# Latent heads scored by pairs with a 32-row rotary product, and banded-layer masks moved to the front of their turn

## The reference

```python
cq, ckv, kr = jnp.split(h @ w_a, [MLA_Q_LORA, MLA_Q_LORA + MLA_KV_LORA], axis=-1)   # 384, 256, 32
cq = rms_norm(cq, g_q); ckv = rms_norm(ckv, g_kv)
q = (cq @ w_uq).reshape(B, L, 16, 64 + 32); q_nope, q_rope = jnp.split(q, [64], axis=-1)
q_rope = apply_rope(q_rope, cos, sin); k_rope = apply_rope(kr[:, :, None, :], cos, sin)
kv = (ckv @ w_ukv).reshape(B, L, 16, 64 + 64); k_nope, v = jnp.split(kv, [64], axis=-1)
qf = concat([q_nope, q_rope]); kf = concat([k_nope, broadcast(k_rope, 16 heads)])
o = dense_causal_attention(qf, kf, v)          # logits over 96 rows, softmax, times v
return o.reshape(B, L, 1024) @ w_o
```

## Time and profile before

| what | value |
|---|---|
| median of 3 runs (lowest to highest) | 1332.93 us (1330.98 to 1333.79) |
| profiled execution: its time, its span | 1333.88 us, 1332.1 us |
| TensorE busy | 1296.4 us, 97% |
| VectorE, ScalarE, GpSimd busy | 938.3, 793.8, 225.8 us |
| TensorE granted clock, mean | 0.995 of full speed |

### The profile page before, as it was taken

The page is one execution under the profiler, slowest core; times in us unless marked ns, Lnnn a source line. Parts: engine busy times, 40 slices in busy tenths (PEclk is TensorE's granted clock), DMA queues, the critical chain, the costliest instruction groups (busy, mean ns, idle before and its releaser), DMA issues.

```text
span 1332.1 us, 29945 instructions
## 1 busy us (share of the span) xinstructions
PE 1296.4 (97%) x10381; PEld 1252.5 (94%) x10381; DVE 938.3 (70%) x1877; ACT 793.8 (60%) x1625; POOL 225.8 (17%) x208
## 2 busy tenths in 40 slices
PE   7999999999998999999998999999999999999997
PEld 7999999999887999999987899999999899999997
DVE  4765877765787877765678687776567667777665
ACT  4565666654565676664476667666446565766643
POOL 1000044420000034330001003433000000244300
PEclk9999999999999999999998999999999999999999
DMA  7432465556421455556442045555645334465562
GB/s 267 140 110 80 143 189 185 178 180 198 133 91 49 130 185 184 180 155 213 155 127 80 33 143 187 187 172 165 208 139 158 111 112 127 144 187 189 174 218 83
DMA packets 56723, 202.80 MB, mean 152 GB/s; under 512 B 6208, under 2 KB 8256, under 8 KB 56512
## 3 DMA queue, kind: packets, MB, share of 16 engines
q1 hardware_dynamic: 56640, 201.68, 47.4%
HBM read 200.61 MB, written 1.05 MB: 151 GB/s over the span
## 4 chain that ended last, share of the span: by engine, by line
PE 82%; DVE 7%; ACT 5%; issue 3%; DMA 1%; POOL 1%; ACTq 0%; DVEq 0%; POOLq 0%; SPq 0%
PE ps L385 23%; PE ps L389 22%; PE ps L388 22%; PE ps L535 2%; PE ps L553 2%; ACT probs L889 2%; DVE w_lo L1260 1%; PE ps L424 1%; PE ps L518 1%; PE ps L430 1%; PE ps L427 1%; ACT w_hi L839 1%; DMA raw<-in_weights 1%; POOL gated L1234 1%; DVE scores L1320 1%
## 5 line engine op out<-in xcount | busy, mean ns | idle before, releaser
L1260 DVE TENSOR_TENSOR w_lo<-raw,w_hi 128x1024 fp32r<-128x1024 f32 x377 | 461.1, 1225 | 230.3 <-ACT w_hi L839 228.9
L385 PE MATMUL ps<-h_hi,w_hi 128*128 128x272 f32 (+1 forms) x1752 | 508.6, 290 | 1.8 <-DVE q_rope L1526 1.0
L389 PE MATMUL ps<-h_hi,w_lo 128*128 128x272 f32 (+1 forms) x1752 | 505.8, 289 | 0.0
L388 PE MATMUL ps<-h_lo,w_hi 128*128 128x272 f32 (+1 forms) x1752 | 499.6, 285 | 0.0
L839 ACT ACTIVATE w_hi<-raw 128x1024 fp32r<-128x1024 f32 x377 | 395.0, 1050 | 147.7 <-PE ps L385 136.9
L385 PEld LDWEIGHTS ps<-h_hi,w_hi 128*128 128x128 f32 x1752 | 329.1, 188 | 8.4 <-issue 5.4
L388 PEld LDWEIGHTS ps<-h_lo,w_hi 128*128 128x128 f32 x1752 | 330.0, 188 | 0.3
L389 PEld LDWEIGHTS ps<-h_hi,w_lo 128*128 128x128 f32 x1752 | 328.9, 188 | 0.0
L385 PE MATMUL ps<-hid_hi,w_hi 128*128 128x272 f32 (+2 forms) x636 | 185.4, 292 | 2.2 <-DVE w_lo L1260 1.9
L388 PE MATMUL ps<-hid_lo,w_hi 128*128 128x272 f32 (+2 forms) x636 | 183.1, 288 | 0.0
L389 PE MATMUL ps<-hid_hi,w_lo 128*128 128x272 f32 (+2 forms) x636 | 183.0, 288 | 0.0
(11 more groups left out here) (184 smaller groups left out, 1727.3 us busy)
## 6 DMA issues: line engine op xcount, KB each, us to landing
raw<-in_weights SPq DMA_DIRECT2D x377, 512.0 KB, 3.7
cst<-in_consts SPq DMA_DIRECT2D x1, 1795.5 KB, 12.1
h<-in_x SPq DMA_DIRECT2D x2, 544.0 KB, 5.8
out<-h SPq DMA_DIRECT2D x8, 128.0 KB, 1.7
```

What stands on the lines that cost most here:

```text
L385: m = pe.matmul(b, whi, xhi, start=n == 0, stop=False)
L388: pe.matmul(b, whi, xlo, start=False, stop=False)
L389: m = pe.matmul(b, wlo, xhi, start=False, stop=n == len(tiles) - 1)
L1260: return dve.tensor_tensor(out_, a_, b_, op)
```

## The change

Latent layer: the nope rows of two heads lie on the two halves of the partitions, as in the other layers; the rotary rows of four heads share one tile, and the rotary key, whose 32 weight columns are laid out four times, lies on all four quarters. A pair's scores are six products of 64 rows and then six of 32 rows added to them. The copies under the heads go away (GpSimd has no part any more), copies by halves become whole ones, the key scale is spread from the per-token column by three small products in place of the ones-product, and the order of the first panels becomes rope, query, key, rope. Fox: `take_k` before the second split of its turn. Swa: masks first, split before `normalise`. Table load: from before the first splits of `down` to after those of its second panel.

```diff
-            def score(a, kind, hn):
-                q, key = queries[0:K_ROWS[kind], hn], keys[0:K_ROWS[kind], hn]
-                if hn >= 2:
-                    pe.wait_ge(masked, h0 + hn - 1)
...
+            def score_latent(a, m):
+                if m:
+                    pe.wait_ge(masked, HEADS * a + 2 * m)
                 for ch, (lo, hi) in enumerate(CHUNKS):
+                    hi_q = max(hi, P)
+                    for s in range(2):
+                        r = slice(HD * s, HD * s + HD)
+                        pe.matmul(ps[0:hi_q - lo, 2 + s, SCOL[ch]:SCOL[ch + 1]], queries[r, m, lo:hi_q],
+                                  keys[r, m, 0:hi], start=ch == 0, stop=False)
+                for ch, (lo, hi) in enumerate(CHUNKS):
+                    hi_q = max(hi, P)
+                    for s in range(2):
+                        t = MLA_ROPE * ((2 * m + s) % 4)
+                        r = slice(t, t + MLA_ROPE)
+                        ins = pe.matmul(ps[0:hi_q - lo, 2 + s, SCOL[ch]:SCOL[ch + 1]],
+                                        queries[r, PAIRS + m // 2, lo:hi_q], keys[r, PAIRS, 0:hi],
+                                        start=False, stop=ch == 2)
+                ins.then_inc(scored, 2)
@@ sum_squares, and after the swap of the rotary key
-                            if not is_q:
-                                pe.matmul(ps[:, 6, 0:T], ones, y[:, k % 4, :], start=k == ks[0], stop=k == ks[-1])
+                    pe.wait_ge(lat_scale, 1)
+                    for n, (lo, hi) in enumerate(((0, P), (P, 2 * P), (2 * P, T))):
+                        ins = pe.matmul(ps[:, 6, lo:hi], lat_col[0:hi - lo, 1, n:n + 1].broadcast_to([hi - lo, P]),
+                                        ident[0:hi - lo, 0:hi - lo], start=True, stop=True)
@@ ScalarE, latent
-                        for s in range(2):
-                            ins = act.activation(queries[0:HD, 2 * m + s, :], bank(p, 2)[HD * s:HD * s + HD], ACT.Copy)
-                        ins.then_inc(q_taken, 1)
+                        act.activation(queries[:, m, :], bank(p, 2), ACT.Copy).then_inc(q_taken, 1)
@@ ScalarE, output
-                if n % 2:
-                    act.preload_act_table_set(TABLES)
...
+                    if k == 1 and n % 2:
+                        act.preload_act_table_set(TABLES)
                     if k:
                         square(n, k - 1)
@@ GpSimd: the four copies of the rotary key are gone
@@ VectorE, fox
                             split_units(a, "qk", 0, 2 * m)
-                            if m == 0:
-                                take_k(m)
+                            take_k(m)
                             split_units(a, "qk", 0, 2 * m + 1)
-                            if m:
-                                take_k(m)
@@ VectorE, swa
-                    split_units(a, "vk", 0, 0)
                     for j in range(2):
                         dve.wait_ge(panel_done, pv + j + 1)
                         vk_evac(0, j, bank(pv + j), pv + j)
+                    split_units(a, "vk", 0, 0)
...
-                        if m >= 4:
-                            out_lo(a, m - 4)
                         if m >= 2:
                             mask_scores(a, kind, 2 * m - 4)
                             mask_scores(a, kind, 2 * m - 3)
                         if 1 <= m <= PAIRS:
                             rope_q(m - 1)
+                        if m >= 4:
+                            out_lo(a, m - 4)
+                        if m < PAIRS:
+                            split_units(a, "q", 0, m)
                         if m >= 2:
                             normalise(a, kind, 2 * m - 4)
                             normalise(a, kind, 2 * m - 3)
                         if m < PAIRS:
-                            split_units(a, "q", 0, m)
                             dve.wait_ge(panel_done, pq + m + 1)
@@ VectorE, mla
-                        for t in range(4):
-                            r = slice(32 * t, 32 * t + 32)
-                            ins = tt(queries[64:96, 4 * m + t, :], y[r, 0, :], y[r, 1, :], ALU.add)
-                        ins.then_inc(roped, 1)
+                        tt(queries[:, PAIRS + m, :], y[:, 0, :], y[:, 1, :], ALU.add).then_inc(roped, 1)
...
-                        tt(keys[0:64, 2 * m, :], b[0:64], kv_rstd[0:64], ALU.mult)
-                        tt(keys[0:64, 2 * m + 1, :], b[64:128], kv_rstd[64:128], ALU.mult).then_inc(bank_free, 2)
+                        tt(keys[:, m, :], bank(p, 2), kv_rstd, ALU.mult).then_inc(bank_free, 2)
...
-                    own.link(dve.reciprocal(kv_rstd, kv_rstd))
...
-                        if m:
-                            normalise(a, kind, 2 * m - 2)
                         if m < PAIRS:
                             take_k(m)
+                        normalise(a, kind, 2 * m - 2)
```

More of the change, by code:

```diff
@@ L266, in build_program @@
             sem(n) for n in ("lat_sq", "lat_sum", "lat_std", "lat_hi", "lat_scale"))
[L267 removed]
+        vt_done, vt_copied, q_taken, lat_spread = (
+            sem(n) for n in ("vt_done", "vt_copied", "q_taken", "lat_spread"))
         conv_begun, silu_done, gate_mul, hid_hi_done, hid_ready = (
@@ L787, in _ @@
                             swap_rope(n // 4)
-                    for r in range(2):
-                        panel(sq, uq, pq, 0, r, from_latent(0), None, 0)
-                    for m in range(PAIRS + 1):
+                    for j, first in ((0, 0), (1, 0), (2, QT)):
+                        panel(sq, uq, pq, 0, j, from_latent(first), None, 0)
+                    pe.wait_ge(q_taken, 1)
+                    panel(sq, uq, pq, 0, 3, from_latent(0), None, 0, pq + 1)
+                    for m in range(1, PAIRS + 1):
                         p = pq + 2 + 2 * m
@@ L1120, in _ @@
                     split_unit(uv + 1 + AHEAD)
[L1121 to L1124, removed]
+                    take_r(2)
+                    split_panel(a, "qk", 0)
+                    take_q(0)
+                    split_panel(a, "qk", 1)
+                    split_panel(a, "qk", 2)
+                    take_r(3)
+                    split_panel(a, "qk", 3)
+                    for m in range(1, PAIRS + 1):
                         if m >= 4:
                             out_hi(a, m - 4)
-                        if m:
-                            exps(a, kind, 2 * m - 2)
+                        exps(a, kind, 2 * m - 2)
                         if m < PAIRS:
                             take_q(m)
-                        if m:
-                            exps(a, kind, 2 * m - 1)
+                        exps(a, kind, 2 * m - 1)
                         if m < PAIRS:
@@ L1212, in _ @@
             for a, kind in enumerate(KINDS):
[L1213 to L1224, removed]
                 norm(2 * a, "o")
@@ L1602, in rope_key_rows @@
                         dve.wait_ge(bank_free, LAYERS[a]["a"][2] + 6)
-                        own.link(tt(scores[0:32, 0, 0:T], gated[0:32, :], cos[0:32], ALU.mult))
+                        one, two = scores[:, 0, 0:T], scores[:, 1, 0:T]
+                        own.link(tt(one, gated[:], cos, ALU.mult))
                         dve.wait_ge(swapped, base)
-                        tt(scores[0:32, 1, 0:T], ps[0:32, 7, 0:T], sin[0:32], ALU.mult).then_inc(roped, 1)
+                        tt(two, ps[:, 7, 0:T], sin, ALU.mult).then_inc(roped, 1)
                         dve.wait_ge(roped, base)
-                        tt(scores[0:32, 0, 0:T], scores[0:32, 0, 0:T], scores[0:32, 1, 0:T],
-                           ALU.add).then_inc(key_roped, 1)
+                        tt(keys[:, PAIRS, :], one, two, ALU.add).then_inc(key_roped, 1)
                     def rope_r(m):
-                        dve.wait_ge(bank_free, pr + m + 1)
+                        dve.wait_ge(bank_free, (pr, pr + 1, pq, pq + 3)[m] + 1)
                         dve.wait_ge(lat_sum, QT + KT)
@@ L1638, in _ @@
                     split_unit(uv + AHEAD)
[L1639 to L1640 removed]
                     rope_r(1)
                     split_unit(uv + 1 + AHEAD)
[L1643 to L1645 removed]
+                    dve.wait_ge(lat_std, 2)
+                    split_units(a, "qk", 0, 0)
+                    take_k(0)
+                    for j in (1, 2, 3):
+                        split_units(a, "qk", 0, j)
+                    for m in range(1, PAIRS + 1):
                         if m == PAIRS:
                             out_lo(a, m - 4)
[L1648 to L1650 removed]
+                        mask_scores(a, kind, 2 * m - 2)
+                        mask_scores(a, kind, 2 * m - 1)
                         if 4 <= m < PAIRS:
                             out_lo(a, m - 4)
[L1653 to L1654 removed]
                         if m < PAIRS:
                             take_k(m)
[L1657 to L1658 removed]
+                        normalise(a, kind, 2 * m - 2)
+                        normalise(a, kind, 2 * m - 1)
                         if m < PAIRS:
```

(6 more changed lines are left out.)

45 lines of the change are left out of this document (15 added, 30 removed).

## The result

| | before | after |
|---|---|---|
| median, us (13 runs each) | 1332.94 (1330.98 to 1335.41) | 1335.36 (1334.52 to 1338.27) |
| profiled execution: time, span | 1333.88, 1332.1 | 1334.52, 1332.3 |
| TensorE, VectorE, ScalarE, GpSimd busy | 1296.4, 938.3, 793.8, 225.8 | 1298.4, 923.9, 790.2, 221.3 |

The ratio is 1.0022, interval 1.0014 to 1.0029: 2.4 us slower against a forecast of 1.8 slower (1334.7). As I wrote, two halves nearly cancel; the stretches between the first matmuls of the four up projections separate them (each holds the MLP of one layer and the mixer of the next, which is named).

What follows compares the result with a forecast made beforehand. TensorE, 82% of the chain, was taken as the bound. Terms 9.6 - 0.4 - 0.8 - 3.0 - 4.5 + 0.9 = +1.8 us, applied to the median 1332.93, gave 1334.7 us; range 1328.5 to 1340.5.

Steps and rivals of the forecast that it cites:

- Banded loop, +9.6: Banded layer: `w_lo` waits for ScalarE's late `w_hi`, so VectorE's turn grows from 7.77 to 9.33 us; 9.6 us slower.
- The clock behind the loop, +0.9: Banded layer: a slow clock stretch after turn 8's idle time shows, at up to 1.8 us; 0.9 slower taken.
- I take half: Banded layer, behind turn 8: half of the possible 1.8 us slow-clock loss counted, 0.9 us.
- second rival: Clock falls in each banded turn, or the last layer's 0.6 us wait still lowers it: 1337 us; chance 0.17.
- Starts of banded and forgetting layers, -0.4 and -0.8: Banded panel copies come behind fewer splits, 0.4 us saved; second forgetting key copy earlier, 0.4 in each of two layers.
- Table load, -3.0: Last layer's down projection: moving the load cuts 1.28 us of TensorE's waiting and 1.7 of slow clock; 3.0 saved.
- I take both: Last down projection: both the 1.28 us shorter wait and the 1.7 us lost to the slow clock counted as gained.
- Latent layer, -4.5: Latent layer: idle time, slow clock and key waits go, against new waits and pairs of 2.15 us; 4.5 us saved.
- The new waits: Latent layer: TensorE waits anew for the query copy, keys and even head's exps; 1.2 us lost.
- The first rival: Latent scores: 32-row products do not overlap or drain the engine, 2.9 us a pair, 1340.7 us; chance 0.18.
- The third rival: Banded loop: the split does not wait as `w_hi` is in time, TensorE bounds turns at 7.35, 1321.3 us; chance 0.05.
- The fourth: Latent layer gives more: 1.8 us a pair, no new waits, no fall of the clock, 1329.8 us; chance 0.14.

Runs made afterwards that it cites:

- the alternation: Changed kernel with each pair's 64-row and 32-row products alternating chunk by chunk instead of six then six: 1339.99 us, ratio 1.0052 to the kernel before.

## Why the prediction was right

**Banded loop, +9.6.** The step that carried the sign held: the place of `w_lo` in VectorE's order, `w_hi` last in ScalarE's, the wait between them, and a turn of 9.33, measured 9.38. Undoing the loop alone gave 10.2 back in the medians, and moving either the split or its input removes the loss. VectorE's wait of 2.4 was forecast as 2.3, TensorE's ahead of the transposes of 1.96 as 1.6. From the first copy to `queries` to the last the loop takes 10.3 us more (50.40 before, 60.72 after), where I had 10.0: four turns of +1.61 and two of +1.94. My own chain of 9.33 would have made it 1.56 and 1.99, not the 1.53 and 1.95 that I took. What follows the last copy gave 0.3 back, forecast 0.4.

**The clock behind the loop, +0.9.** The mechanism is real, the size was too large. In both profiles of the changed kernel the term is nothing: the layer took 9.48 us more in both, where my terms for it sum to 10.1. In one of five profiles with this loop the clock fell behind turn 8's wait and cost 1.17, in four it cost nothing or nearly so; that is 0.2 on average, with few profiles to say it from. The step that was mis-sized is "I take half": in two of the five a fall one turn earlier had already shortened turn 8's wait. Of the second rival half came true, the clock fell in the loop, in one profile three times and in the other once, but the fall lay in time that TensorE would have idled. Its other half, a fall behind the last layer's 0.6 us, did not come in the trace of the changed kernel.

**Starts of banded and forgetting layers, -0.4 and -0.8.** The first copy to `queries` comes 11.78 us behind the layer's first matmul, 12.31 before: -0.53. The forgetting layers gave 0.33 and 0.36. All three are near, and the cover for the later split and masks held, as no new wait stands in the list.

**Table load, -3.0.** In the profiled executions 2.84. Near there, yet mis-sized for a median: the step "I take both" counted a slow stretch as if every execution had it, and at 1.7 where it cost 1.1. Alone the move gave about 1 us. It is the largest error against the medians, and would account for a change that is 2.4 slower there and 1.0 in the two profiles; this last step is argued, as no median can be divided into stretches.

**Latent layer, -4.5.** Measured -4.95, and -4.9 alone in the medians, with two errors that cancel. The pair was taken at 2.15 and is 2.25, 8 x 0.1 more. Twice the banded 1.13 was right, but the hand-over of 0.1 that I took off it is not there. The new waits were taken at 1.2; the list has one of 0.3 for queries, and TensorE is busy 19.56 of 20 us where they should lie. A remaining 0.3 is not placed.

**The first rival** was half right, and I had tied two things together that come apart. The 32-row products do overlap, wholly; changing the height does cost, 0.15 to 0.18. The rule that I cited against the change ("TensorEngine Tiling (Array Packing)", Key Properties, in the Trainium skill) is borne out by the alternation so far as a price shows at each change; it did not move the pair towards the upper end of 2.9. (The 1.13 that I doubled comes from 64-row products between 128-row ones, and so may already hold the price of a change; that is argued.) The pair of 2.25 lies just under the 2.26 from which I let this rival decide. The third rival did not occur, since `w_hi` is late as the rows said. The fourth's absent waits and absent fall of the clock occurred, its 1.8 a pair did not. (The chances of cases 3 and 4 sum to 0.19 and those of 1 and 2 to 0.35, not to 0.18 and 0.36.)

**The sum.** That it came within 0.7 us of the median is in part luck. The loop and its sign were understood; but the clock's term and the latent layer's made the forecast 0.9 and 0.4 too slow, and the loop's and the table load's made it 0.4 and some 2 us too fast, the last against the medians.

## What to carry to other kernels

Moving an instruction forward on one engine moves nothing if its input is the last thing another engine makes in that turn; what stood behind it then waits as well. Look up where the producer stands before you move the consumer, and move either both or neither: here the split behind the normalisations, with the masks first, gives 1324.35 us, faster than both kernels.

Two short products side by side on parts of the array cost here what one product of 96 rows costs (0.94 us against 0.90 for three), plus 0.15 to 0.18 us each time the height changes, so group the products of one height. Cutting one head of 96 rows into 64 and 32 for two heads at once is no gain in itself: a pair went from 1.80 to 2.25 us, and the layer gained by the copies and waits that went away.

And a slow stretch of the clock that one profile shows behind a wait may be worth less than its full price in a median: look in a second profile whether it is there again. Behind the table load it came in one of three, in the latent layer in three of three, and inside a loop that another engine bounds it cost nothing, except behind the loop's last wait.

## What the runs showed that I had not expected

Whether the granted clock falls behind a given wait varies from execution to execution. In the banded loop of the changed kernel waits of 1.95 to 2.33 us were followed by a fall three times out of three in one profile and once out of five in the other. And the wait of 1.91 us in the last layer was followed by 0.57 over 4 us, waits of 2.01 and 1.88 at the same place in two kernels with the same last down projection by 1.00.

And the matmuls' pace varies where the granted clock does not. The last up projection took 117.68 us in the first profile of the changed kernel and 119.25 in the second, both without a longer wait. A window of 30 us inside it, the second profile first:

```profile
1190.00:1220.00 30.00, 30.00 (x251) 30.00 (x250) 22.70 (x34) 19.16 (x32) 11.96 (x11) 1.00 0.56 180
```

```profile
1190.00:1220.00 30.00, 30.00 (x254) 30.00 (x254) 22.77 (x33) 18.37 (x32) 12.76 (x11) 1.00 0.61 185
```

251 matmuls in place of 254, at a clock of 1.00 in both. The profile of the kernel with the odd head's products left out shows the same 119.25 us, the ten others 117.68 to 117.72. What slows them stays open; it is 1.6 us in one stretch, more than several terms of the prediction.
